# Two-layer hybrid encoder on one core: weight buffers in another order, other issue points for expert weights, and two loads cut into sixteen

## What is computed

```
for layer in (0, 1):
    proj = rmsnorm(h) @ w_in[layer]                  # 1024 -> 2048: u, q, k, v
    y_pool = pool_mixer(u)                           # window means over tokens, then pool_w
    y_na   = neighbourhood_attention(q, k, v, rpb)   # 16 heads
    h = h + rmsnorm(concat(y_pool, y_na) @ w_out[layer])
    hn = rmsnorm(h)
    if layer == 0:  f = (silu(hn @ wg) * (hn @ wu)) @ wd      # dense, 1024 -> 4096 -> 1024
    else:           f = top-2-of-8 experts, each (silu(x @ w_gate[e]) * (x @ w_up[e])) @ w_down[e]
                                                              # 1024 -> 3584 -> 1024
    h = h + rmsnorm(f)
```

## Time and profile before

| | us |
|---|---|
| median of three runs | 1308.23 (1307.15 to 1308.72) |
| the profiled execution | 1306.5 |
| its span, first to last instruction | 1304.7 |
| TensorE busy in it | 1256.1 (96%) |
| VectorE, ScalarE, GpSimd busy | 403.4, 284.6, 109.2 |
| moved by DMA | 443.44 MB |

### The profile page before, as it was taken

How to read it: one execution, slowest core, us unless ns; L and a number is a source line. 1 busy time by engine, 2 the same in 40 slices (tenths; PEclk the granted TensorE clock), 3 DMA queues, 4 the chain that set the end, 5 groups by cost and what they waited for, 6 DMA issues and landing times.

```text
span 1304.7 us, 30033 instructions
## 1 busy us (share of the span) xinstructions
PE 1256.1 (96%) x13883; PEld 777.7 (60%) x13883; DVE 403.4 (31%) x560; ACT 284.6 (22%) x430; POOL 109.2 (8%) x240
## 2 busy tenths in 40 slices
PE   9999999999999999999999999999999779999976
PEld 8888999999989863443453364353354244345324
DVE  5876554545476860200310030210030030031011
ACT  5666433344465640001001000001000000100101
POOL 3334300000000307300000000000000000000000
PEclk9999999999999999999999999999999999999999
DMA  9637765565553669999999999999999999999994
GB/s 303 222 118 235 229 249 195 187 238 185 179 212 130 235 271 427 425 426 425 425 424 426 425 425 425 427 424 426 424 424 425 427 425 425 425 425 425 424 425 201
DMA packets 67152, 443.44 MB, mean 340 GB/s; under 512 B 4536, under 2 KB 10816, under 8 KB 42448
## 3 DMA queue, kind: packets, MB, share of 16 engines
q1 hardware_dynamic: 64880, 433.58, 81.8%
q0 software_dynamic: 2144, 7.90, 2.0%
HBM read 439.36 MB, written 2.10 MB: 338 GB/s over the span
## 4 chain that ended last, share of the span: by engine, by line
PE 80%; DMA 14%; DVE 3%; ACT 1%; SPq 1%; issue 0%; ACTq 0%; DVEq 0%
PE psum L1085 30%; PE psum L1094 15%; DMA unit<-in_moe_w_down 10%; PE psum L740 9%; PE psum L742 9%; PE psum L741 9%; DMA unit<-in_moe_w_up 3%; PE psum L1029 1%; PE psum L1040 1%; PE psum L837 1%; DMA ring<-in_w_in 1%; PE psum L828 1%; SPq L389 1%; PE psum L854 1%; PE psum L769 1%; DVE hs L1541 1%
## 5 line engine op out<-in xcount | busy, mean ns | idle before, releaser
L1085 PE MATMUL psum<-unit,xT 128*32 128x448 f32 x5120 | 487.4, 541 | 15.9 <-DMA unit<-in_moe_w_up 15.2
L1085 PEld LDWEIGHTS psum<-unit,xT 128*32 128x32 f32 x5120 | 163.4, 110 | 334.6 <-issue 302.5
L1094 PE MATMUL psum<-unit,hid 128*32 128x256 f32 x4480 | 248.7, 380 | 14.2 <-DMA unit<-in_moe_w_down 13.0
L1094 PEld LDWEIGHTS psum<-unit,hid 128*32 128x32 f32 x4480 | 143.7, 110 | 117.0 <-DMA unit<-in_moe_w_down 17.6
L1760 DVE TENSOR_TENSOR hidp<-hid,psum 128x448 f32<-128x448 f32 x40 | 36.5, 911 | 528.7 <-PE psum L1085 528.7
L740 PE MATMUL psum<-hT_hi,w_hi 128*128 128x256 f32 x656 | 184.8, 282 | 0.1
L1442 DVE TENSOR_TENSOR ring_lo<-ring,w_hi 128x2048 fp32r<-128x2048 f32 x64 | 149.0, 2336 | 114.4 <-ACT w_hi L1204 114.2
L742 PE MATMUL psum<-hT_hi,ring_lo 128*128 128x256 f32 x656 | 183.6, 280 | 0.0
L741 PE MATMUL psum<-hT_lo,w_hi 128*128 128x256 f32 x656 | 183.6, 280 | 0.0
L1204 ACT ACTIVATE w_hi<-ring 128x2048 fp32r<-128x2048 f32 x71 | 135.0, 1909 | 55.7 <-PE psum L742 51.8
L742 PEld LDWEIGHTS psum<-hT_hi,ring_lo 128*128 128x128 f32 x656 | 125.2, 191 | 0.0
(11 more groups left out here) (255 smaller groups left out, 943.6 us busy)
## 6 DMA issues: line engine op xcount, KB each, us to landing
unit<-in_moe_w_gate SPq DMA_DIRECT2D x64, 1792.0 KB, 40.3
unit<-in_moe_w_up SPq DMA_DIRECT2D x64, 1792.0 KB, 39.5
unit<-in_moe_w_down SPq DMA_DIRECT2D x63, 1792.0 KB, 40.4
ring<-in_dense_w_gate SPq DMA_DIRECT2D x8, 2048.0 KB, 9.1
ring<-in_dense_w_up SPq DMA_DIRECT2D x8, 2048.0 KB, 8.9
ring<-in_dense_w_down SPq DMA_DIRECT2D x8, 2048.0 KB, 7.8
ring<-in_w_in SPq DMA_DIRECT2D x6, 2048.0 KB, 8.4
ring<-in_w_out SPq DMA_DIRECT2D x4, 2048.0 KB, 8.2
```

The source lines that it names most:

```text
L1085: ins = mm(bank(half, s)[quad(j)], xT[:, s, dt, :], w[:, at:at + FJ], start=dt == 0, stop=dt == DT - 1)
L1094: ins = mm(down_out[s][quad(j)], e[:, half, s, t, :], w, start=half == t == 0 and s != 2, stop=half == 1 and t == FT - 1, skip_group_check ...
```

## The change

Three things are changed.

First, the order of the buffers in memory. Behind `ring0` and `vv` now come `prob_b`, `pt23`, `uT` and `win_a`, then `ring1`, `w_hi` and `ring2`, then `h`. With that unit 5 lies over the end of `ring0`, `vv` and `prob_b`; unit 6 over `pt23`, `uT` and `win_a`; unit 7 over `ring1`; unit 8 over the end of `ring1` and the first half of `w_hi`; units 9 and 10 over the rest of `w_hi` and `ring2`. The rounded copy of half 70 (`HALF_OUT`) is not written to its stage of `w_hi` but over `prob`, after `turned` has reached 16.

Second, SyncE's waits for units 5 to 10. Unit 5 now waits for `pv_done` alone, unit 6 for the pooling differences, units 7 and 8 for `half_done` 70, units 9 and 10 for `half_done` 72. Units 2 to 4 and 11 and later are issued as before.

Third, units 110 (an up unit of item 4) and 160 (a down unit of item 6) are each loaded by sixteen transfers of eight partitions, where the others are one transfer of 128 partitions. They count on a semaphore of their own, and TensorE waits for it.

The diff:

```diff
--- before.py
+++ after.py
@@ -56,6 +56,7 @@
 MIX_LOADS = 6
 DENSE_LOADS = 3 * DBLOCKS
 MOE0 = 2 * MIX_LOADS + DENSE_LOADS
+HALF_OUT = 2 * MOE0 - 2
 EARLY_UNITS = (8, 16)
 SHIFT = 64
 UNIT = FE
@@ -85,7 +86,9 @@
 LAST_CUT = UNIT - D
 SLOT_OF = [n % SLOTS for n in range(N_UNITS - 1)] + [0]
 assert N_UNITS % SLOTS == 0 and H_SLOT not in SLOT_OF[N_UNITS - SLOTS + H_SLOT:]
-LOADS = [SLOT_OF[:n].count(SLOT_OF[n]) + 1 for n in range(N_UNITS)]
+EIGHT = (110, 160)
+SIXTEEN = [slot if n not in EIGHT else None for n, slot in enumerate(SLOT_OF)]
+LOADS = [SIXTEEN[:n].count(SLOT_OF[n]) + 1 for n in range(N_UNITS)]
 TAKEN = [max([m for m in range(n) if SLOT_OF[m] == SLOT_OF[n]], default=-1) for n in range(N_UNITS)]
 assert UNITS % EXTRA_SLOTS == 0 and HALF_UNITS * UNIT == FT * D
 
@@ -139,14 +142,15 @@
         sb("shift", [P, SHIFT // 4])
         ring = [sb("ring0", [P, 8 * C4])]
         vv = sb("vv", [P, NT, C4])
-        ring += [sb(f"ring{k}", [P, 8 * C4]) for k in range(1, RING)]
-        ring_lo = [sb(f"ring_lo{k}", [P, 8 * C4], F32R, over=f"ring{k}") for k in range(RING)]
-        w_hi = sb("w_hi", [P, STAGE, 8 * C2], F32R)
         prob_b = sb("prob_b", [P, 2, 4, ROWS, COLS])
+        pt23 = sb("pt23", [P, 2, D])
         uT = sb("uT", [P, 4, S + 2 * POOL_PAD])
         win_a = sb("win_a", [P, S + 2 * POOL_PAD])
-        pt23 = sb("pt23", [P, 2, D])
-        sb("gap", [P, (addr["early"] + 4 * UNIT * H_SLOT - plan_top[0]) // 4])
+        sb("gap", [P, (addr["early"] + 4 * UNIT * 7 + SHIFT - plan_top[0]) // 4])
+        ring += [sb("ring1", [P, 8 * C4])]
+        w_hi = sb("w_hi", [P, STAGE, 8 * C2], F32R)
+        ring += [sb("ring2", [P, 8 * C4])]
+        ring_lo = [sb(f"ring_lo{k}", [P, 8 * C4], F32R, over=f"ring{k}") for k in range(RING)]
         h = sb("h", [P, NT, D])
         gpost = sb("gpost", [P, D])
         router_sb = sb("router_sb", [P, DT, Q])
@@ -157,10 +161,11 @@
         hT_hi = sb("hT_hi", [P, DT, S], F32R)
         hT_lo = sb("hT_lo", [P, DT, S], F32R)
         gpre = sb("gpre", [P, D])
+        prob = sb("prob", [P, 2, 4, ROWS, COLS])
         cst = sb("cst", [P, K_ALL])
         st = sb("st", [P, 64])
 
-        prob = sb("prob", [P, 2, 4, ROWS, COLS])
+        w_hi_end = sb("w_hi_end", [P, 8 * C2], F32R, over="prob")
         poolw = sb("poolw", [P, 4, P])
         ypT_lo = sb("ypT_lo", [P, 4, S], F32R)
         delta = sb("delta", [P, 4, S])
@@ -258,7 +263,8 @@
 
             seq, c = n // 2, n % 2
             by_rows = rows_first(seq)
-            hi = w_hi[:, n % STAGE, :].rearrange("p (t n) -> p t n", t=2 if by_rows else DT)
+            hi = w_hi_end[:, :] if n == HALF_OUT else w_hi[:, n % STAGE, :]
+            hi = hi.rearrange("p (t n) -> p t n", t=2 if by_rows else DT)
             return half_of(ring[seq % RING], c, by_rows), hi, half_of(ring_lo[seq % RING], c, by_rows)
 
         def rows_first(seq):
@@ -274,6 +280,7 @@
         half_landed = [sem(f"half_landed{i}") for i in range(2)]
         w_landed = [sem(f"w_landed{i}") for i in range(RING)]
         unit_landed = [sem(f"unit_landed{i}") for i in range(SLOTS)]
+        eight_landed = sem("eight_landed")
         unit_done = sem("unit_done")
         hi_ready = sem("hi_ready")
         first_hi = sem("first_hi")
@@ -428,10 +435,13 @@
         def unit_slot(i, u):
             return SLOT_OF[i * UNITS + u] if isinstance(i, int) else u % EXTRA_SLOTS
 
+        def unit_number(i, u):
+            return i * UNITS + u if isinstance(i, int) else None
+
         def unit_loads(i, u):
             if isinstance(i, int):
                 return LOADS[i * UNITS + u]
-            return (i - NE) * EXTRA_TURNS + (SLOT_OF.count(u % EXTRA_SLOTS) + u // EXTRA_SLOTS + 1)
+            return (i - NE) * EXTRA_TURNS + (SIXTEEN.count(u % EXTRA_SLOTS) + u // EXTRA_SLOTS + 1)
 
         def ends(i):
             return i * 2 - 6
@@ -498,6 +508,10 @@
                 if isinstance(i, int) and (i, u) == (NE - 1, UNITS - 1):
                     sp.dma_start(units[slot][:, 0:LAST_CUT], src[:, 0:LAST_CUT]).then_inc(unit_landed[slot], 16)
                     sp.dma_start(units[slot][:, LAST_CUT:UNIT], src[:, LAST_CUT:UNIT]).then_inc(last_landed, 16)
+                    return
+                if unit_number(i, u) in EIGHT:
+                    for p in range(0, P, 8):
+                        sp.dma_start(units[slot][p:p + 8, :], src[p:p + 8, :]).then_inc(eight_landed, 16)
                     return
                 sp.dma_start(units[slot][:, :], src).then_inc(unit_landed[slot], 16)
 
@@ -519,14 +533,16 @@
             sp.wait_ge(half_done, MH - 4)
             load_unit(0, zeroth, 4)
             sp.wait_ge(pv_done, GROUPS * DEPTH)
-            sp.wait_ge(half_done, MH - 2)
             load_unit(0, zeroth, 5)
-            sp.wait_ge(half_done, MH)
-            for u in range(6, 10):
-                load_unit(0, zeroth, u)
             sp.wait_ge(delta_ready, 3 * DEPTH)
             sp.wait_ge(delta_dve_ready, DEPTH)
-            load_unit(0, zeroth, 10)
+            load_unit(0, zeroth, 6)
+            sp.wait_ge(half_done, MH - 2)
+            for u in (7, 8):
+                load_unit(0, zeroth, u)
+            sp.wait_ge(half_done, MH)
+            for u in (9, 10):
+                load_unit(0, zeroth, u)
             sp.wait_ge(h_parked, 16 * NT)
             sp.wait_ge(hs_ready, 2 * 4)
             sp.wait_ge(logits_done, 1)
@@ -1076,7 +1092,10 @@
             def expert_item(i, groups, before, after, first=False, last=False, extra=False):
 
                 def landed(u):
-                    pe.wait_ge(unit_landed[unit_slot(i, u)], unit_loads(i, u) * 16)
+                    if unit_number(i, u) in EIGHT:
+                        pe.wait_ge(eight_landed, 2 * P * (EIGHT.index(unit_number(i, u)) + 1))
+                    else:
+                        pe.wait_ge(unit_landed[unit_slot(i, u)], unit_loads(i, u) * 16)
 
                 def project_tokens(dt, u, half, s):
                     w = units[unit_slot(i, u)]
@@ -1198,7 +1217,9 @@
                         act.wait_ge(half_landed[seq], 16)
                     elif c == 0 or seq < 2:
                         act.wait_ge(w_landed[seq % RING], 16 * (seq // RING + 1))
-                    if k >= STAGE:
+                    if k == HALF_OUT:
+                        act.wait_ge(turned, GROUPS * DEPTH)
+                    elif k >= STAGE:
                         act.wait_ge(half_done, k - STAGE + 1)
                     src, hi, _ = halves(k)
                     act.activation(hi, src, ACT.Copy).then_inc(hi_ready, 1)
```

## The result

The changed kernel is slower: 1341.77 us median (1337.73 to 1343.22, four runs) against 1307.81 (1307.15 to 1308.72, four runs), a ratio of 1.0256 with a 95% interval of 1.0238 to 1.0273. The forecast was 1298.7, so the miss is 43 us, and it has the wrong sign. The profiled execution has a span of 1340.7.

What follows compares the result with a forecast made beforehand. The prediction took the unit-load DMA stream plus a tail as the bound. From the profiled 1306.5 it took 6.0 for buffers and issue points and 3.5 for balance, giving 1297.0, with 1.7 added back 1298.7 us; range 1295.5 to 1305.

Steps and rivals of the forecast that it cites:

- Units 110 and 160 in sixteen loads: Loading these two units in pieces shifts packets between engine halves, so the stream ends earlier: -3.5 us, bounds -6 and +8.6.
- the lag that the prediction had found: At the stream's end eight engines run on after the other eight stop: 14.6 us by the mean, 12.6 last to last.
- the side: Which eight engines take the eight-row loads: early ones end the stream earlier, late ones move the end by +8.6 us.
- rival A: Units 110 and 160: the eight rows fall on the late eight engines, lag about 30, 1310.8 us, slower; chance 0.15.
- B: Units 110 and 160: the sixteen loads take turns over all 16 engines, no shift between halves, 1302.2 us; chance 0.09.
- D: Early gain lost through a longer gap ahead of unit 12 or a late parking store, only balance left: 1304.7 us; chance 0.05.
- C: Units 110 and 160: the pieces clog the queue, the stream stands some 4.5 us, twice: 1307.7 us; chance 0.05.
- Buffers and issue points: Units 5 to 10 issued earlier make the stream continuous sooner: gain 6.0 us, bounds 0 and 12.9.
- Half 70's copy: Its copy over `prob` waits on ScalarE behind a copy that already waits for the same event: cost 0.
- The range and the chances: Whole kernel: 1295.5 to 1305 us; chances faster 0.80, same 0.12, slower 0.08.

Runs made afterwards that it cites:

- e2: The kernel before with only units 110 and 160 as sixteen loads of eight neighbouring partitions each: 1346.93 us, ratio 1.0311.
- e12: Loads-only kernel, the same four units cut in different ways: 64 rows 2 apart 427 GB/s, 64 neighbours 214, eight neighbours 82.
- e14: Second loads-only kernel, source and destination row orders varied; eight units with the fifth in four loads: 41.3 us for 32 neighbours, 36.1 for rows 4 apart.
- e9: The kernel before with units 110 and 160 each in two loads of 64 neighbouring rows: 1332.1 us, ratio 1.0183.
- e3: The kernel before with units 110 and 160 as sixteen loads of eight rows each, every fourth row: 1336.73 us, ratio 1.0224.
- e4: The kernel before with units 110 and 160 as eight loads of sixteen neighbouring rows each: 1334.16 us, ratio 1.0207.
- e13: The kernel before with units 110 and 160 each in four loads of 32 rows four apart: 1307.58 us, ratio 1.0002.
- e11: The kernel before with units 110 and 160 each in four loads of all 128 rows and a quarter of the columns: 1307.58 us, ratio 1.0004.
- e1: The changed kernel without the sixteen-piece loads, all units as one load, new buffer order and issue points kept: 1301.7 us, ratio 0.9958 to the kernel before.
- e15: The changed kernel with four loads of 32 rows four apart replacing the sixteen loads: 1301.59 us, ratio 0.9961 to the kernel before.
- e8: The kernel before with units 110 and 160 as four loads of 32 neighbouring rows each: 1335.23 us, ratio 1.0204.

## Why the prediction was wrong

**Units 110 and 160 in sixteen loads: the step that failed.** It was put at -3.5 us, and the measured price is +39 (e2), or 1341.8 - 1301.7 = +40 in the changed kernel. Two things in it were wrong.

First, it counted packets and took the duration of each from the stream of whole units. "A row of a unit is one packet" is right, and so is that a load of eight rows lies on eight engines: the share of 0.51 in e12 shows it. But the duration isn't a property of a packet. It depends on which rows are written at the same time: eight neighbours are the worst of the eleven ways in e12, and the packets of the whole units beside them are slowed as well. This term is the large one, about 13 us a unit. From the windows above it is 13 for unit 110; the same subtraction for the three rows of unit 160, 134 + 205 + 125 = 464, gives 11, and more is lost before and after them. Row cuts that keep all 16 engines evenly loaded show it by itself: +23 to +27.

That it is 13 and not the 5.2 of e14 goes with the lag that the prediction had found. In the kernel the late engines reach the cut unit when the early ones have passed it: in e9 half of unit 110's 32 landings come in 926.2 to 934.9 and the other half in 940.4 to 950.4, and the trace has double packet times in 921 to 933 and again in 937 to 948, about 12 and 11 us, at half rate some 6 us lost in each. So all engines are slowed twice, once for each half. No run took the lag away, so that the lag doubles the price is read from traces and not tested.

Second, the side: the eight rows fall on neither half but on six early engines and two late ones. The prediction had set two cases, all early or all late, and a set that lies across both has the price of the late side, since a unit counts when its last engine is through: rival A's mechanism, for two engines. It can be read apart from the half rate in the traces. In e2 the windows 900 to 960, 1120 to 1150 and 1150 to 1200 have 331, 418 and 294 GB/s; what is missing to 425 is (94 x 60 + 7 x 30 + 131 x 50) / 425 = 29 us, and 39 - 29 = 10 is left for this, where A had 8.6. In e3, the other kernel with loads of eight rows, the same windows have 357, 420 and 337 GB/s, which is 20 us, and 29 - 20 = 9 is left. Both have the two engines that run on alone (share 0.12 to 0.15), and behind unit 110 their landings come as two, twelve and two; in e4, whose loads have 16 rows, they still come as eight and eight, and the same sum for e4 gives 26 us, its whole price. So e3's spread rows did spare some of the half rate, which its total hides. No run changed this part by itself.

**Rivals.** A had the small part of the loss; the half rate is in none of the four. B and D are out. C looked in the right place, the 50 us after 890 and 1110, for the wrong sign, a hole in the DMA share. SyncE needed 19.2 and 21.1 us for the sixteen issues, not the 5.3 of the prediction, but the share stays at 1.0, and e13 shows that the queue takes four pieces of a unit at no cost. The sentence of the Trainium skill, page "DMA: Bandwidth & Descriptors", section "Bandwidth", on "Batch DMAs to ≥1 MiB" had the right sign for another reason: loads of 0.46 MB cost nothing in e11 and e13. (The 2.0 us that the prediction takes from there stand in the same page's section "Anatomy of one DMA — SWDGE (gpsimd) path".)

**Buffers and issue points: right.** Forecast -6.0, measured -6.1 in e1 and -5.6 in e15. The shares are as forecast (1.00 in 454 to 462 and in 467.4 to 472, 0.00 in 494 to 496). Unit 12 was expected at 500.9 to 501.9. It landed at 504.1 in the profile after, for its issue came 3 us later than before, at 496.8; in e1 at 502.4 and in e15 at 500.4, with issues at 495.2 and 492.6. What goes with it is TensorE's clock during its first unit. Of e15 first, then of the profile after:
```profile
488.00:492.00 4.00, 4.00 (x46) 2.19 (x46) 1.44 (x7) 0.00 (x0) 1.37 (x6) 1.00 0.89 373
492.00:496.00 4.00, 4.00 (x48) 1.37 (x44) 0.00 (x0) 0.00 (x0) 3.21 (x12) 1.00 0.69 205
```
```profile
488.00:492.00 4.00, 4.00 (x26) 2.61 (x22) 1.44 (x7) 0.00 (x0) 0.28 (x2) 0.50 0.98 330
492.00:496.00 4.00, 4.00 (x28) 1.06 (x24) 0.00 (x0) 0.00 (x0) 3.11 (x12) 0.50 0.32 133
```
At full clock TensorE gets through 46 and 48 products in these 4 us, at half (1.2 GHz) 26 and 28, and unit 12's buffer comes free later.

**Half 70's copy: right.** e1 carries it and has the whole gain; the profile shows no new wait at the mixing.

**The range and the chances.** A total of 0.08 for slower was too little. The doubtful term had its bounds, -6 and +8.6, from rows in which every load had all 128 rows. Such rows can't bound what a load with other rows does. That queued loads bear no extra price was argued from "in the stream one follows every 4.3", which is a row of whole units; no row showed it for parts.

## What to carry to other kernels

Where a load is cut, cut it by columns, or into 64 rows 2 apart or 32 rows 4 apart in SBUF, so that every piece still reaches rows all over the 128. Neighbouring rows halve the rate of all 16 engines, or worse, and of the whole loads next to them. The step alone is not enough: eight rows 4 apart lie within 32 rows, and cost 29 us (e3). Before an operation's price is taken from rows of the trace, ask whether these have the same shape as the new one, and when several variants all cost the same, ask what they have in common before ruling it out. And read GB/s beside the DMA share: a share of 1.0 with half the bytes is a stall inside the transfers.

## What the hardware showed that was not expected

- A load of 64 rows into neighbouring SBUF rows runs at 214 GB/s, into rows 2 apart at 427; the order of the source is without effect (215 against 428 with the sides changed over).
- One unit cut into neighbouring rows costs 5.2 us in a stream of eight, and 25 to 27 us for two in this kernel (e4, e8, e9), where transfers of other units are slowed with it: 374 packets over 0.7 us around unit 110 in e9, of which the unit itself has at most 128.
- Sixteen landings count for a load on eight engines: TensorE's wait for 256 per unit is met by sixteen such loads, though the trace has only nine updates of the semaphore for each (288 for 32 loads in e2).
- The 16 engines fall into two halves that drift apart in a long stream: 0.5 us at 495, 8 us at 914, 14.3 us at the end of it, in the kernel before. That instruction loads feed this lag is the prediction's guess; no run tested it.
- The reordered kernels scatter more: 1299.8 to 1306.7 in ten runs of e1 and 1299.8 to 1307.0 in eight of e15, where the kernel before stays within 1306.2 to 1309.9 in nineteen. Unit 12 now follows TensorE's first unit without a backlog behind which a late clock could hide; the profiled executions (unit 12 at 500.4 with 1300.2 us, at 502.4 with 1302.7) agree with that, which is two points and no test.
